# Latent attention heads and their output projection in one block, with one buffer for gate and output

## The reference, cut to what matters

```python
q = jnp.einsum("bsc,chd->bshd", c_q, w_uq)          # 8 heads, 128 + 64 wide
q_nope = q[..., :QK_NOPE]
q_rope = apply_rope(q[..., QK_NOPE:], cos[None, :, None], sin[None, :, None])
...
    s = jnp.einsum("bqhd,bkhd->bhqk", qn_b, k_nope)
    s = s + jnp.einsum("bqhr,bkr->bhqk", qr_b, k_rope)
    s = jnp.where(mask[None, None], s * ATTN_SCALE, -jnp.inf)
    p = jax.nn.softmax(s, axis=-1)
    return jnp.einsum("bhqk,bkhd->bqhd", p.astype(v.dtype), v)
...
y = o.reshape(bsz, seq, N_HEADS * V_DIM) * jax.nn.silu(gate)
return y @ w_out                                     # x = x + this; then two norms
```

## Time and profile before

| | |
|---|---|
| median of three executions | 2742.04 us |
| profiled execution, its own time | 2739.2 us |
| its span, first to last instruction | 2737.4 us |
| TensorE busy | 2523.7 us, 92% of the span |
| VectorE busy | 1569.6 us, 57% |
| ScalarE busy | 1198.8 us, 44% |
| GpSimd busy | 191.3 us, 7% |
| mean granted TensorE clock | 0.969 of full |
| DMA | 206.79 MB, mean 76 GB/s |

### The profile page before, as it was taken

How to read it: one execution, slowest core, us unless ns; L and a number is a source line. 1 busy time by engine, 2 the same in 40 slices (tenths; PEclk the granted TensorE clock), 3 DMA queues, 4 the chain that set the end, 5 groups by cost and what they waited for, 6 DMA issues and landing times. The chain is left out here.

```text
span 2737.4 us, 32268 instructions
## 1 busy us (share of the span) xinstructions
PE 2523.7 (92%) x12061; PEld 2072.5 (76%) x12061; DVE 1569.6 (57%) x2881; ACT 1198.8 (44%) x2061; POOL 191.3 (7%) x114
## 2 busy tenths in 40 slices
PE   5999598998999979899999997999899998999987
PEld 3777487876777767688888885878778786888866
DVE  6655556434555546666666665453466554666664
ACT  4555433223444434455555554341444434454442
POOL 0000011000000025000000000000112120000012
PEclk9999899999999999999999998999899999999998
DMA  2212331112222132111011110224443420011133
GB/s 106 75 50 75 132 105 64 62 62 85 93 67 72 62 123 85 31 39 34 29 39 39 39 39 18 78 96 153 152 135 131 146 85 27 32 46 38 39 127 108
DMA packets 89830, 206.79 MB, mean 76 GB/s; under 512 B 7136, under 2 KB 39776, under 8 KB 88672
## 3 DMA queue, kind: packets, MB, share of 16 engines
q1 hardware_dynamic: 89696, 204.98, 22.7%
HBM read 163.99 MB, written 40.96 MB: 75 GB/s over the span
## 5 line engine op out<-in xcount | busy, mean ns | idle before, releaser
L197 PE MATMUL acc<-operand_hi,w_hi 128*128 128x512 f32 x1846 | 750.0, 406 | 56.3 <-DVE w_lo L192 11.9
L199 PE MATMUL acc<-operand_hi,w_lo 128*128 128x512 f32 x1846 | 729.2, 395 | 0.0
L198 PE MATMUL acc<-operand_lo,w_hi 128*128 128x512 f32 x1846 | 727.8, 394 | 0.0
L197 PEld LDWEIGHTS acc<-operand_hi,w_hi 128*128 128x128 f32 x1846 | 352.4, 191 | 141.4 <-issue 39.0
L199 PEld LDWEIGHTS acc<-operand_hi,w_lo 128*128 128x128 f32 x1846 | 351.0, 190 | 77.2
L198 PEld LDWEIGHTS acc<-operand_lo,w_hi 128*128 128x128 f32 x1846 | 352.5, 191 | 68.6 <-issue 2.4
L192 DVE TENSOR_TENSOR w_lo<-w_raw,w_hi 128x1024 fp32r<-128x1024 f32 (+1 forms) x209 | 234.1, 1120 | 222.8 <-ACT w_hi L186 222.2
L186 ACT ACTIVATE w_hi<-w_raw 128x1024 fp32r<-128x1024 f32 (+1 forms) x209 | 202.7, 970 | 358.0 <-PE aux L199 171.6
L197 PE MATMUL aux<-operand_hi,w_hi 128*128 128x512 f32 x634 | 261.0, 412 | 54.3 <-DVE out_a_w2l L763 27.9
L198 PE MATMUL aux<-operand_lo,w_hi 128*128 128x512 f32 x634 | 251.5, 397 | 0.0
L199 PE MATMUL aux<-operand_hi,w_lo 128*128 128x512 f32 x634 | 251.4, 397 | 0.0
(11 more groups left out here) (404 smaller groups left out, 4201.0 us busy)
## 6 DMA issues: line engine op xcount, KB each, us to landing
w_raw<-in_stream SPq DMA_DIRECT2D x209, 512.0 KB, 3.7
ssd_e<-cs_scratch SPq DMA_DIRECT2D x8, 1024.0 KB, 7.0
g_scratch<-ssd_work SPq DMA_DIRECT2D x12, 512.0 KB, 2.9
ssd_xbc<-g_scratch SPq DMA_DIRECT2D x8, 768.0 KB, 4.9
y_scratch<-rnn_y SPq DMA_DIRECT2D x10, 512.0 KB, 3.0
out_a_raw<-y_scratch SPq DMA_DIRECT2D x20, 256.0 KB, 5.6
resid<-in_x SPq DMA_DIRECT2D x8, 512.0 KB, 7.3
g_scratch<-mlai_g SPq DMA_DIRECT2D x8, 512.0 KB, 2.9
```

What stands on the lines that cost most here:

```text
L197: pe.matmul(out, w_hi, x_hi, start=first, stop=False)
L198: pe.matmul(out, w_hi, x_lo, start=False, stop=False)
L199: return pe.matmul(out, w_lo, x_hi, start=False, stop=last)
```

## The change

The two stages share one block: `latent_attention` makes the heads' programs and the projection's and hands both to `together`, so that each engine goes on from one to the other without a barrier. The first half of y is loaded, split and multiplied for tiles 0 and 1 inside the last head. Its four buffers are the two halves of the rotation table (free after head 7's rotation) and of `vt` (free once v is turned); the last block is taken from y itself. `y` is now the buffer `g`: the output overwrites the gate, and SP stores it, waits for the store, and then loads the next gate. The rotation writes both products into `t12` (two rows of buffers instead of one), and the accumulator is freed after the second product, ahead of the add. DVE makes the output ahead of the normalisation in rounds 3, 5 and 7. The second projection tile's weights are split in head 6. The projection keeps its squares in rings of two, in buffers of the heads.

Most of the textual difference is indentation; this is the difference without it.

```diff
-        mla_heads(k, ka, kb, rope)
-    with ExitStack() as c:
-        together(k, project_halves(k, c, "out_b", 0, DT, "a2"))
+        with ExitStack() as c:
+            heads, begun, own = mla_heads(k, c, ka, kb, rope)
+            together(k, heads, project_halves(k, c, "out_b", 0, DT, "a2", begun=begun, own=own))
...
-    vt, v, g, y = (sb(n, [P, S]) for n in ("vt", "v", "g", "y"))
-    t12 = sb("t12", [64, S])
+    vt, v, g = (sb(n, [P, S]) for n in ("vt", "v", "g"))
+    y = g
+    t12 = sb("t12", [64, 2, S])
...
+    begun = Begun(k, "mla_out", 0, [bank(rope, n) for n in range(2)] + [bank(vt, n) for n in range(2)],
+                  (bank(k.acc[:, 0, :], 0), bank(k.acc[:, 0, :], 1)))
+    block = Stage()
...
+            if b == last:
+                sp.wait_ge(s["rb"], MLA_HEADS)
+                for d in range(2):
+                    begun.load(sp, d)
             if b:
                 sp.wait_ge(s["y"], 4 * b)
-                sp.dma_start(g[:, :], k.g_dram[b]).then_inc(s["gate"], 16)
                 sp.dma_start(k.y_dram[b - 1], y[:, :]).then_inc(s["stored"], 16)
+                sp.wait_ge(s["stored"], 16 * b)
+                sp.dma_start(g[:, :], k.g_dram[b]).then_inc(s["gate"], 16)
+            if b == last:
+                sp.wait_ge(s["vtr"], 2 * MLA_HEADS)
+                for d in range(2, MLA_HEADS - 1):
+                    begun.load(sp, d)
+                begun.load_rest(sp)
...
+                if not more and t:
+                    begun.part(pe, t - 1)
...
                     rest()
                     if more:
                         scores(b + 1, 0)
+                    else:
+                        begun.part(pe, t)
...
-            act.wait_ge(k.acc_free[tile("r", b).slot], tile("r", b).before + 1)
-            act.activation(qa[0:64, b % 2, :], t12[:, :], ACT.Copy).then_inc(s["qah"], 1)
+            act.wait_ge(s["rb"], b + 1)
+            act.activation(qa[0:64, b % 2, :], t12[:, 0, :], ACT.Copy).then_inc(s["qah"], 1)
...
+                if not more:
+                    if t < 7:
+                        begun.high(act, t)
+                    if t == 6:
+                        act.wait_ge(s["y"], 4 * b + 2)
+                        begun.high(act, 7, bank(y, 0))
...
-                    if b + 2 < MLA_HEADS:
                         split("r", b + 2)
...
-            dve.tensor_tensor(t12[:, :], acc[64:128, :], rope[64:128, :], ALU.mult).then_inc(s["ra"], 1)
-            dve.tensor_tensor(acc[0:64, :], acc[0:64, :], rope[0:64, :], ALU.mult).then_inc(s["rb"], 1)
+            dve.tensor_tensor(t12[:, 1, :], acc[64:128, :], rope[64:128, :], ALU.mult).then_inc(s["ra"], 1)
+            dve.tensor_tensor(t12[:, 0, :], acc[0:64, :], rope[0:64, :], ALU.mult).then_inc(k.acc_free[t.slot], 1)
             dve.wait_ge(s["ra"], b + 1)
-            dve.wait_ge(s["rb"], b + 1)
-            dve.tensor_tensor(t12[:, :], acc[0:64, :], t12[:, :], ALU.add).then_inc(k.acc_free[t.slot], 1)
+            dve.wait_ge(k.acc_free[t.slot], t.before + 1)
+            dve.tensor_tensor(t12[:, 0, :], t12[:, 0, :], t12[:, 1, :], ALU.add).then_inc(s["rb"], 1)
...
-                if t < 7:
-                    norm(b, t + 1)
                 if t in (3, 5, 7):
                     output(b, t // 2 - 1)
+                if t < 7:
+                    norm(b, t + 1)
...
                 if t + 2 < QT:
                     maximum(b, t + 2)
+                if not more:
+                    if t < 7:
+                        begun.low(dve, t)
+                    if t == 6:
+                        begun.low(dve, 7, bank(y, 0))
...
-                    if t == 6 and b + 2 < MLA_HEADS:
+                    if t == 6:
                         split("r", b + 2)
...
+    own = {"raw": begun.raw, "ring": 2, "sq": v[:, :].rearrange("p (n c) -> p n c", c=HALF),
+           "sq2": g[:, :].rearrange("p (n c) -> p n c", c=HALF), "squares": ((s["stored"], 16 * MLA_HEADS),),
+           "tmp": pth[1][:, :, :].rearrange("p (n a) q -> p n (a q)", n=4),
+           "sum2": pth[0][:, 0:4, :].rearrange("p a q -> p (a q)"),
+           "free": ((s["pv"], 4 * MLA_HEADS), (begun.s["lo"], DT))}
+    return block, begun, own
```

More of the change, by code:

```diff
@@ L1284, with mla_heads @@
 MLA_ROWS = {"v": 0, "k": 1, "q": 2, "r": 3}
-def mla_heads(k, ka, kb, rope):
+def mla_heads(k, c, ka, kb, rope):
     nc = k.nc
@@ new lines, in sb @@
+    def sb(name, shape, dt=F32):
+        return c.enter_context(nc.sbuf_tensor("mlah_" + name, shape, dt))
+    q2, k2 = sb("q2", [P, 2, S], F32R), sb("k2", [P, 2, S], F32R)
+    qh, ql = (k.xh[:, 5, :], q2[:, 0, :]), (k.xl[:, 5, :], q2[:, 1, :])
+    kh, kl = (k.xh[:, 6, :], k2[:, 0, :]), (k.xl[:, 6, :], k2[:, 1, :])
+    qa = sb("qrope", [P, 2, S], F32R)
+    vt, v, g = (sb(n, [P, S]) for n in ("vt", "v", "g"))
+    y = g
+    t12 = sb("t12", [64, 2, S])
+    pth = [sb("pth0", [P, QT - 2, QG]), sb("pth1", [P, QT, QG])]
@@ new lines, in mla_heads @@
+    probs = (k.stat_sq, k.stat_diag)
+    begun = Begun(k, "mla_out", 0, [bank(rope, n) for n in range(2)] + [bank(vt, n) for n in range(2)],
+                  (bank(k.acc[:, 0, :], 0), bank(k.acc[:, 0, :], 1)))
+    block = Stage()
+    slots, out_v = (bank(k.acc[:, 1, :], 0), bank(k.acc[:, 1, :], 1)), k.acc[:, 1, HALF:HALF + QG]
+    first = {"v": k.acc[:, 0, :], "r": k.acc[:, 1, :], "q": k.aux[:, 0, :], "k": k.aux[:, 1, :]}
+    shapes = {"v": (KV_KT, Q_KT), "k": (KV_KT, Q_KT), "q": (Q_KT, 0), "r": (Q_KT, 0)}
@@ new lines, in mla_heads, with tile, width, proj @@
+    last = MLA_HEADS - 1
+    def tile(name, b):
+        return Tile(j0, 4 * b + MLA_ORDER.index(name), 2, 0)
+    def width(name, b):
+        return shapes[name][0] * P if b < MLA_HEADS else DT * P
+    def proj(name, b):
+        return k.acc[:, 0, :] if b else first[name]
+    @block.sync
+    def _(sp):
+        def load(n):
+            t = Tile(j0, n, 2, 0)
+            row = 4 * (n // 4) + (MLA_ROWS[MLA_ORDER[n % 4]] if n < 4 * MLA_HEADS else n % 4)
+            sp.wait_ge(k.w_lo[t.slot], t.before)
+            sp.dma_start(k.w_raw[:, t.slot, :], k.stream[row0 + row]).then_inc(k.w_loaded[t.slot], 16)
+        sp.dma_start(g[:, :], k.g_dram[0]).then_inc(s["gate"], 16)
+        for n in range(2, 6):
+            load(n)
+        for b in range(MLA_HEADS):
+            if b == last:
+                sp.wait_ge(s["rb"], MLA_HEADS)
+                for d in range(2):
+                    begun.load(sp, d)
+            if b:
+                sp.wait_ge(s["y"], 4 * b)
+                sp.dma_start(k.y_dram[b - 1], y[:, :]).then_inc(s["stored"], 16)
+                sp.wait_ge(s["stored"], 16 * b)
[5 more added lines that the diff above has]
+                begun.load_rest(sp)
+            if b < last:
+                for n in range(4 * b + 6, 4 * b + 10):
+                    load(n)
+        sp.wait_ge(s["y"], 4 * MLA_HEADS)
+        sp.dma_start(k.y_dram[last], y[:, :]).then_inc(s["stored"], 16)
+        sp.wait_ge(s["stored"], 16 * MLA_HEADS)
```

574 lines of the change are left out of this document (268 added, 306 removed).

## The result

The changed kernel takes 2712.49 us (median of 4 executions, 2709.96 to 2715.8), the kernel before 2742.93 in the same session: a ratio of 0.9894, interval 0.9882 to 0.9906. The profiled execution's span is 2708.2 us (before 2737.4), its mean granted clock 0.973 (before 0.969).

The account below looks back on a forecast made before the run. PE was taken to bound the heads and DMA the projection's fill. -5.4 (rotation, shared buffer) - 5.5 (output) + 0.8 (split) + 13.8 (last head) - 20.6 (way to tile 2) = -16.9 us: 2725 from 2742.0; range 2714 to 2736.

Parts of the forecast that it names:

- Term 1: Rotation in the heads: accumulator freed by the second product, so PE's whole wait of 1.18 us goes, seven times: 8.3 us.
- term 2: SP's gate load behind the store's landing: weights 1.3 us late, leaving the rotation -5.4 us (bounds -8.3 and -1.2).
- a wait of ACT's split of over 1 us: Sign of a right forecast: ACT's split waits more than 1 us for the weights in six heads.
- heads near 41.3: Sign of a right forecast: heads 1 to 5 take near 41.3 us each.
- weights 2 us later: Rival on SP's chain of loads: the rotation gains nothing in six heads, sum -13 us, total 2729; chance 0.14.
- Output: Round 5 of seven heads: output ahead of normalisation comes 0.79 us earlier, within PE's wait: -5.5 us.
- Split in head 6: DVE in head 6: one 1.22 us weight split ahead of round 7's output, partly in idle time: +0.8 us (0 to 1.2).
- Last head: Last head: 48 projection matmuls add 10.8 us, PE's waits on low operands leave 9.8 us idle: +13.8 us.
- a throttled last head: Rival: three fifths of the last head at 1.2 GHz, 14 us lost instead of 3.4; -6, 2736; chance 0.08.
- Last head to tile 2: From last output to projection tile 2: 25.5 us becomes 3.7, with 1.2 lost to half clock: -20.6 us.
- all of it comes through: Rival: weights in time, last head and tile 2 at full clock; -24.4 us, total 2717.6; chance 0.15.
- The other side: Rival: SP's store, gate and weights land strictly in turn, q weights 6.2 us late; +12, 2754; chance 0.04.

Follow-up runs that it names:

- the merge alone: The changed kernel with the rotation in PSUM and the output behind the normalisation, both as before; 2725.47 us, ratio 0.9938.
- the run with the low half first: The changed kernel with an operand's low half made ahead of the row maximum in rounds 1 to 5 of the last head; 2710.41 us, ratio 0.9891.
- the two holds: The changed kernel with useless VectorE work between projection and next stage, 0.96 us or about 2.4 us; 2716.72 and 2724.10 us.
- a hold: The kernel before with a useless VectorE add of 0.96 us at the end of its projection block; 2739.86 us, ratio 0.9991.

## Why the prediction was right or wrong

**The step that failed** is the term that the sum put at nothing: the 1600 us of unchanged code behind the projection. No reason was given why they should keep their length, and they took 6.4 us less in the profiled execution, with 84.5 us at 1.2 GHz instead of 98.1. The parts that were in the sum gave -22.9, which alone would have been 2742.0 - 22.9 = 2719, inside the range; the stretch behind took it out below. Of the parts in the sum one was clearly mis-sized, the rotation behind the shared buffer, by 3.8 us. Term by term:

1 and 2. **Rotation and shared buffer: mis-sized, -5.4 forecast, -9.2 measured** (1.31 a head, seven heads). Term 1 was right (the whole wait goes; even its own bound of 1.18 a head was 0.13 too small). The mechanism of term 2, the wait for the landing, is there to the tenth (2.6 us), and its price was wrong: I let the weights keep most of the 6.2 us that they took beside gate and store, and chose 1.3 us late "nearer to the upper end". They took 4.4 from issue to split once the store was out of their way, which gives back 1.8 of the 2.1 us by which they are issued later (2.97 behind the head's first issue instead of 0.85); the remaining 0.3 was idle time ahead of the rotation. The lower bound of my own bracket (0 late) was nearly right, and of the signs that I named, a wait of ACT's split of over 1 us and heads near 41.3, neither came: the wait is 0.56, the heads take 40.65. The Trainium skill (DMA: Bandwidth & Descriptors, "Anatomy of one DMA") gives one transfer on the GpSimd path a fixed part that doesn't shrink with its size. The trace, on SP's queue, is not against it, since the store's landing, 2.6 us, is paid; but what I concluded from it for the chain, weights 2 us later and nothing gained by the rotation in six heads, did not come: the rotation gained everything.

3. **Output: right.** -5.5 forecast, 0.78 a head in the run alone, times seven 5.5. PE's wait fell to 0.2 at most, as forecast.

4. **Split in head 6: +0.8 forecast, +0.6 measured** in the merge alone (44.21 against 43.60).

5. **Last head: +13.8 forecast, +12.4 measured.** The idle time of PE is 47.00 - 37.77 = 9.2 us, forecast 9.8, and the six waits on low operands are 1.28, 1.57, 1.00, 1.84, 0.45 and 2.10 where 1.4, 1.7, 1.0, 2.0, 0.4 and 2.3 were worked out, from rows of before alone. The wait ahead of round 7's values is 0.58 (forecast 1.0). The clock is 0.96 instead of the 0.90 that was kept. The opposite rival, a throttled last head, fell: holes of 0.5 to 2.1 us between groups of matmuls left the granted clock at 0.96 and, in the merge alone, at 1.00. The Trainium skill (TensorE: Matmul & The Clock Gate, "A second HAM failure mode") reports of another kernel that short idles between groups of matmuls let the clock swing. This last head shows one fall and no swing: the clock went to 1.2 GHz at 963.3 us, behind the longest wait (2.10), and in the merge alone the same wait was followed by none.

6. **Last head to tile 2: -20.6 forecast, -20.8 measured** up to the next stage's first load, and that this is so near is luck in part, as two misses cancel: 25.5 us became 3.0 (-22.5 where -21.8 were forecast; the 0.5 added for POOL's clearing wasn't there, the operand took 0.69), and from tile 2 on the projection is 1.7 us longer, where 1.2 were put for the first tile at half clock. The clock stood at 1.2 GHz from 980.4 to 983.8 us.

**Behind the projection: 0 forecast,** -6.4 us in the profiled execution; the rests of the two medians, -7.7 and -5.0, agree with it in size. The rival "all of it comes through" was nearest (-24.4), by one of its three reasons: the weights were in time, but the last head stood at 0.96 and tile 2 began at half clock.

The other side, SP's chain as the bound of a head, fell: it asked for weights 6.2 us late, and they were 0.3 late.

**Shown:** the parts one by one (the runs with one part each, which add up in the middle heads), the cause of the last head's waits (the run with the low half first brings them from 8.2 to 2.2 us), and that a delay of 1 to 2 us ahead of unchanged stages changes their length by more than itself (the two holds in the changed kernel, in one session). **Open:** what start gives which length. The stretch began at 1101.3, 1103.2, 1104.4 and 1105.5 us in four executions of nearly the same kernel and took 1606.9, 1609.3, 1607.0 and 1616.2; the kernel before began it at 1124.2 and 1127.4 and took 1613.2 and 1619.8, and with a hold at 1127.6 and took 1610.5. The start within the span doesn't order them; the time at 1.2 GHz nearly does. The largest rest, -10.1 of the merge alone, is -5.2 of this stretch and 5.5 by which the median of before in that session (2744.72) lies above the profiled execution of before (2739.2). Why one of its four executions took 9.6 us more than the others stays open.

## What to carry to other kernels

When a transfer is put behind the landing of another, it leaves behind the traffic that slowed it: price the later start against the faster transfer; here the two cancelled, and the wait that was feared was free. In a kernel with long unchanged stages that spend some time at 1.2 GHz, an edit ahead of them can change how much: don't put them at nothing, widen the range by what executions of one kernel differ by in that stretch (here some 6 us), and judge a part by its own stretch of the trace, never by the total alone. Where a matrix product waits for an operand in a softmax loop, try its place by a round: one round later here took all six waits away, and 8.4 us off the last head.

## What the runs showed of the hardware

- Of 1.2 GHz: in the stretch of identical code the fourteen profiled executions had 84.5 to 111.8 us of it and took 1606.9 to 1619.8 us, a bit under 0.5 us longer for each us more (12.9 over 27.3). A hold of 2.4 us ahead of it cost 11.5 in all, one of about 1 us in the kernel before nothing that shows. The Trainium skill (TensorE: Matmul & The Clock Gate, "What's actually happening") says that the gate's watching runs freely and isn't reset when a kernel starts, so that the point of a transition varies. The profiled executions of the kernel before, with 98.1 and 111.8 us at 1.2 GHz in the same code, are in line with it, but no run here shows that this is the cause.
- 512 KB of weights from issue to landing: 5.7 to 6.7 us as the first of two loads beside a gate and a store of the same size, 4.2 to 4.5 beside the gate without the store (six heads each).
- VectorE beside GpSimd: a subtraction of two buffers took its usual 0.69 while POOL cleared a buffer (977.67), and one of 1.22 took 1.70 while POOL added (983.49). The Trainium skill (SBUF — State Buffer, "SBUF: two separate sides") has the two engines exclude each other only if VectorE has two inputs on chip and GpSimd reads there too; both rows agree, as clearing reads nothing and POOL's add reads two buffers. By that rule the 0.5 us for the clearing would not have been in term 6.
